# Squares of the out-projections summed on GpSimd, open stage borders and a third weight place in a three-block transformer kernel

## The chip, the cores and the metric

The kernel runs on one core of a Trainium2 chip. The metric is the device time of one execution in microseconds, from its first to its last instruction and what lies around them. Three runs of the kernel before gave 3401.47, 3403.77 and 3406.58 us; their median is 3403.77 us.

## The reference

The program computes two models one after the other on 256 latent tokens of width 2048, in float32. The first has two layers. A layer normalises latent and context tokens (256 each), scales and shifts them by a modulation made from a small vector, projects them by `w_in`, runs grouped-query and latent attention, gates both with a silu, and projects back:

```python
for l in range(DEPTH):
    shift, scale, gate = jnp.split(sc @ w_ada[l] + b_ada[l], 3, axis=-1)
    h_lat = rms_norm(x, norm_g[l]) * (1.0 + scale[:, None]) + shift[:, None]
    ...
    x = x + gate[:, None] * merge_groups(o_a, lat_a[3], o_b, lat_b[3], w_out[l])
return rms_norm(x, final_g)
```

The second model has one layer: a hybrid mixer (forgetting attention and a linear recurrence) with its own out-projection, then an expert layer that picks 128 of 16384 experts for each token. Each norm divides by the root of the mean of the squares over all 2048 channels. Channels lie on the partitions, so that mean is a sum over partitions and over 16 chunks.

## The kernel before

**Stages.** `stages` is a list that every engine walks in the same order. For the first model a layer is: scale, norm, the in-projection (37 weight panels of 1 MB), the grouped attention, the up-projection (7 panels), the latent attention, the out-projection (16 panels). Layer 0 works on 512 columns (context and latent); layer 1 keeps context only where keys and values need it, so most of its outputs have 256 columns. At the start of a stage `begin` (L666) makes an engine wait until the other compute engines have ended all stages before it; each ends a stage with a drain that counts up `done`.

**A weight panel.** SyncE loads it into one of two ring places of 8 KB a partition (`SLOTS`, later six, when the modulation has left its buffers). A panel is split for accuracy: ScalarE rounds half a panel (`act_half`, L1334, instruction at L1345), VectorE subtracts to get the remainder (`dve_half`, L1347, instruction at L1351). There are four places for such halves. TensorE then multiplies hi·hi, hi·lo and lo·hi, 48 matmuls for an output (`pe_output`, L1066, matmuls at L1090). `paced` (L1318) lets ScalarE and VectorE run some halves ahead of the output that they take next. A ring place is free when VectorE has subtracted its second half; SyncE waits for that and issues the next load (L734).

**Modulation.** The products with `w_ada` are done on VectorE, one 1 MB chunk of weights at a time (L1819, 2.3 us each), beside the projections; `ada_after` says how many chunks come behind which output. GpSimd issues their loads into two places (L872) in a hardware loop.

**Norm statistics of an out-projection.** When VectorE has added an output to the residual (L1873), ScalarE squares it into one of two places of `sq` (L1401, or L1394 where two norms are fused and each chunk is squared twice). TensorE multiplies each by a matrix of ones and adds them in PSUM (`sum_squares`, L977, matmuls at L996, or L987 where fused), two outputs behind. There are three such stages: the out-projections of layer 0 (512 columns, 16 sums), of layer 1 (256 columns, fused, 32 sums) and of the second model (256 columns, 16 sums).

**The border behind them.** ScalarE loads an activation table (L1493), takes the root (L1478, L1479), and rounds four weight halves of the next projection before its norm work; VectorE scales each chunk (L1957, or L1955), modulates every fourth itself (L1964), and puts four half subtractions between them; remainders (L1939) run four chunks behind. TensorE starts the next projection with `pe_pair` (matmuls at L1061), two outputs interleaved, each chunk as its remainder is ready.

**Gates.** The last 16 outputs of an in-projection are gates. ScalarE writes each into `sq` place 2 (L1425), stores it to DRAM (L1427) and waits for that store before it writes the next. At the stage's end it waits for all stores.

## Time and profile before

| what | value |
|---|---|
| runs, median | 3403.77 us |
| profiled execution, its own time | 3404.52 us |
| its span | 3402.8 us |
| mean granted clock of TensorE | 0.954 of 2.4 GHz |
| TensorE busy | 89% of the span |
| VectorE, ScalarE, GpSimd busy | 73%, 35%, 18% |
| DMA | 932.69 MB, mean 274 GB/s |

The busy share of TensorE counts overlapping matmuls once, so 89% says that it seldom stands still, not that it runs at its peak. In time, layer 0 lasts to about 1000 us, layer 1 to 1625 us, the mixer and its out-projection to 2037 us, and the expert layer takes the rest.

### The profile page before, as it was taken

The page shows a single profiled execution, that of the slowest core. Times are in us where ns is not written, and L with a number is a line of the kernel's source. Part 1 is how long each engine was busy: PE and PEld are TensorE (multiplying, and loading weights), DVE is VectorE, ACT ScalarE, POOL GpSimd, SP SyncE. Part 2 cuts the span into 40 slices and gives each one's busy share as a digit, 9 for nine tenths or more (in the row PEclk, how much of TensorE's full clock was granted, in tenths as well). Part 3 has the DMA queues.
Part 4 walks back from the last instruction along what each step waited for, and adds up shares of the span by engine and source line. Part 5 has one row for each costly group of instructions (what it writes and reads, how often), then busy time and mean ns, then how long its engine had stood idle before and what let it go on. Part 6 is the DMA issues. An engine that isn't in the chain of part 4 may idle for free.

```text
span 3402.8 us, 39344 instructions
## 1 busy us (share of the span) xinstructions
PE 3036.7 (89%) x14780; PEld 2316.8 (68%) x14780; DVE 2477.8 (73%) x3460; ACT 1174.2 (35%) x1805; POOL 610.7 (18%) x692
## 2 busy tenths in 40 slices
PE   5899999999988998999899999899999997757566
PEld 1577887556767887659899899788888885222223
DVE  7888996655766776547664545598988997888886
ACT  1332323323233333234554635344444443111111
POOL 1000000000100000000000000122122223777773
PEclk9999999999999999999899998999999998878888
DMA  9554674343765676427544444599999999999996
GB/s 407 199 197 183 246 261 174 136 173 139 301 241 222 235 299 258 176 109 283 213 155 145 160 161 151 222 412 419 401 420 399 417 398 381 370 409 409 409 409 264
DMA packets 149479, 932.69 MB, mean 274 GB/s; under 512 B 21552, under 2 KB 30000, under 8 KB 40880
## 3 DMA queue, kind: packets, MB, share of 16 engines
q0 software_dynamic: 77568, 520.24, 39.0%
q1 hardware_dynamic: 57616, 384.82, 28.8%
q10 hardware_dynamic: 14112, 25.17, 1.9%
q8 instruction: 118, 1.93, 0.2%
q14 instruction: 65, 0.53, 0.0%
HBM read 900.79 MB, written 29.36 MB: 273 GB/s over the span
## 4 chain that ended last, share of the span: by engine, by line
PE 56%; DVE 14%; DMA 11%; PEld 7%; issue 6%; POOL 4%; ACT 2%; SPq 0%; DVEq 0%; PEldq 0%; POOLq 0%; ACTq 0%
PE psum L1090 22%; PE psum L1037 16%; PEld psum L1090 7%; PE psum L1099 5%; DMA memh<-dots,memr 4%; DVE w_lo L1351 3%; PE psum L1229 3%; DMA memr<-in_panels_dram 3%; DVE psum L2270 2%; POOL memh L891 2%; PE psum L1246 2%; POOL memr L903 2%; PE psum L1061 2%; DVE junk L1819 2%; DMA memh<-in_panels_dram 1%
## 5 line engine op out<-in xcount | busy, mean ns | idle before, releaser
L1351 DVE TENSOR_TENSOR w_lo<-memr,w_hi 128x1024 fp32r<-128x1024 f32 x614 | 737.0, 1221 | 380.2 <-ACT w_hi L1345 379.6
L1345 ACT ACTIVATE w_hi<-memr 128x1024 fp32r<-128x1024 f32 x614 | 641.0, 1056 | 938.2 <-PE psum L1090 330.9
L1090 PE MATMUL psum<-h_hi,w_hi 128*128 128x512 f32 (+1 forms) x1632 | 587.6, 360 | 19.8 <-DVE w_lo L1351 19.7
L1819 DVE CUSTOM_DVE_ANT_0 junk<-memr 128x2048 bf16<-128x2048 f32 x224 | 512.2, 2287 | 87.4 <-DMA memr<-in_ada_dram 67.1
L1090 PE MATMUL psum<-h_hi,w_lo 128*128 128x512 f32 (+1 forms) x1632 | 563.9, 346 | 0.0
L1090 PE MATMUL psum<-h_lo,w_hi 128*128 128x512 f32 (+1 forms) x1632 | 563.3, 345 | 0.0
L1268 PE MATMUL psum<-memr,memh 128*128 128x512 f32 x576 | 312.6, 702 | 193.1 <-ACT memh L1755 175.7
L1037 PE MATMUL psum<-w_hi,l_hi 128*128 128x512 f32 x1024 | 401.1, 392 | 12.5 <-DVE w_lo L1351 12.4
L1037 PE MATMUL psum<-w_hi,l_lo 128*128 128x512 f32 x1024 | 399.9, 391 | 0.0
L1037 PE MATMUL psum<-w_lo,l_hi 128*128 128x512 f32 x1024 | 399.8, 390 | 0.0
L1268 PEld LDWEIGHTS psum<-memr,memh 128*128 128x128 f32 x576 | 126.0, 226 | 379.3 <-ACT memh L1755 189.3
L1090 PEld LDWEIGHTS psum<-h_hi,w_hi 128*128 128x128 f32 x1632 | 312.0, 191 | 70.2 <-issue 22.1
L1090 PEld LDWEIGHTS psum<-h_lo,w_hi 128*128 128x128 f32 x1632 | 311.9, 191 | 44.9 <-issue 8.8
L872 POOL DMA_DIRECT2D memr<-in_ada_dram x160 | 84.5, 528 | 1433.7 <-DVE mod L1822 1412.7
L1090 PEld LDWEIGHTS psum<-h_hi,w_lo 128*128 128x128 f32 x1632 | 311.6, 191 | 37.1
L2270 DVE SCALAR_TENSOR_TENSOR psum<-memr,memh,psum 128x2048 f32<-128x2048 f32 x118 | 277.9, 2355 | 9.3 <-DVE memr L2207 0.2
L1090 PE MATMUL psum<-l_hi,w_hi 128*128 128x256 f32 x848 | 243.0, 287 | 0.0
L1090 PE MATMUL psum<-l_lo,w_hi 128*128 128x256 f32 x848 | 240.1, 283 | 0.0
L1090 PE MATMUL psum<-l_hi,w_lo 128*128 128x256 f32 x848 | 240.1, 283 | 0.0
L1037 PEld LDWEIGHTS psum<-w_hi,l_hi 128*128 128x128 f32 x1024 | 193.2, 189 | 55.5 <-DVE w_lo L1351 12.6
L882 POOL DMA_INDIRECT memr<-in_peer_u_dram,memr x64 | 76.0, 1188 | 838.7 <-issue 586.7
L1037 PEld LDWEIGHTS psum<-w_lo,l_hi 128*128 128x128 f32 x1024 | 193.1, 189 | 40.2
(273 smaller groups left out, 4475.3 us busy)
## 6 DMA issues: line engine op xcount, KB each, us to landing
memr<-in_panels_dram SPq DMA_DIRECT2D x323, 1024.0 KB, 7.3
memr<-in_ada_dram POOLq DMA_DIRECT2D x168, 1024.0 KB, 6.0
memh<-in_panels_dram SPq DMA_DIRECT2D x16, 1024.0 KB, 23.6
dots<-sq ACTq DMA_DIRECT2D x64, 256.0 KB, 10.0
memh<-in_ada_dram POOLq DMA_DIRECT2D x8, 1024.0 KB, 15.9
memr<-in_xin_dram SPq DMA_DIRECT2D x1, 4096.0 KB, 40.9
gstore<-sq ACTq DMA_DIRECT2D x16, 256.0 KB, 4.8
memh<-gstore SPq DMA_DIRECT2D x2, 2048.0 KB, 7.3
```

The costliest lines, as they stand in the source:

```text
L872: pool.dma_start(adar[:, s_, :], ada[i * 2 + s_]).then_inc(ada_in[s_], 16)
L882: pool.indirect_dma_start(out=early_rows[:, r % EARLY_SLOTS, :], out_offset=None, in_=(peer_u if j < TOPK else peer_v)[:, :], in_offset=ba ...
L891: pool.indirect_dma_start(out=late_act[:, m, j:j + 1], out_offset=None, in_=dots[:, :], in_offset=bass.IndirectOffsetOnAxis(ap=eidx[:, EAR ...
L1037: ins = pe.matmul(bank(2 * (group % 2) + t), x_[:, kc, t * P:t * P + P], u_[:, c, :], start=kc == 0 and j == 0, stop=kc == DC - 1 and j == 2)
L1090: ins = pe.matmul(bank(o["bank"])[:, 0:o["w"]], w_[:, c, :], x_[:, kc, :], start=kc == 0 and j == 0, stop=kc == DC - 1 and j == 2)
L1099: ins = pe.matmul(bank(o["bank"])[:, a:b], lt, rh, start=j == 0, stop=j == len(pairs) - 1)
L1229: ins = pe.matmul(b[:, 0:nk], lt, rh, start=j == 0, stop=j == len(u["s"]) - 1)
L1268: ins = pe.matmul(bank(b), diags[:, q % DIAGS, :], row_views[r % NSLOT][:, 512 * b:512 * b + 512], start=first and i == 0, stop=(EARLY + m ...
L1345: act.activation(w_hi[:, m % HALVES, :, :], slot[:, 8 * i:8 * i + 8, :], ACT.Copy).then_inc(hi_ready, 1)
L1351: dve.tensor_tensor(w_lo[:, m % HALVES, :, :], raw_panel(o["g"])[0][:, 8 * i:8 * i + 8, :], w_hi[:, m % HALVES, :, :].bitcast(F32), ALU.su ...
L1819: chain(dve.tensor_tensor_reduce(junk[:, :], w, cact[:, v_, :], 1.0, 0.0, ALU.mult, ALU.add, mod[:, a, m:m + 1]))
L2270: dve.scalar_tensor_tensor(sums_dve, row, by, sums_dve, ALU.mult, ALU.add).then_inc(row_added, 1)
```

## The change

1. **Squares.** ScalarE writes the squares of the first output straight into `sq` place 2, and GpSimd adds those of outputs 1 to 14 onto them. TensorE sums over partitions twice a norm: the total, and the last output's squares. GpSimd's loop of modulation loads is written out, with the additions placed between the loads.
2. **Borders.** ScalarE and VectorE no longer wait for other engines' `done` at a scale or norm stage behind an out-projection; no engine does at the grouped attention (single semaphores take its place), nor TensorE at an out-projection. Three of the four halves of the next projection are split during the out-projection; one to three halves of an out-projection are split during the latent attention before it (one in layer 0, three in layer 1). The table load moves to the start of the out-projection. VectorE modulates chunks 0, 4, 8, 12 in place of 1, 5, 9, 13, and the remainder of chunk 0 comes behind chunk 2.
3. **Third place.** In layer 1's in-projection, panels go round three places. The third is the context half of `q`, 8 runs of 1 KB a partition, free once the norm has read all of X.
4. **Gates** of 256 columns alternate between the two halves of `sq` place 2; the wait for all stores at the end goes. **Modulation** chunks of layer 1's in-projection are spread anew (the same 42).

```diff
+        for j in range(37):
+            slot_of[first_1 + j] = ((first_1 % SLOTS, (first_1 + 1) % SLOTS, SPARE)[j % 3])
+        spare = region(AR, 8, T2)[:, :, 0:S]
...
-        spread(DC + 60, 42, [0.6] * 2 + [2] * 3 + [0.7] * 12 + [2] * 4 + [0.8] * 14 + [0] * 2)
+        for j, n in enumerate([1, 1, 2, 2, 2] + [1, 1, 0, 1, 1, 1, 1, 1] + [1] * 4 + [2] * 4 + [1] * 15 + [0]):
+            ada_after[DC + 60 + j] = n
...
+            if me in ("act", "dve") and st.get("seam"):
+                upto = 0
+            if me != "sp" and "follows" in st or me == "pe" and "after_split" in st:
+                upto = 0
...
+                    elif slot_of[i] == SPARE:
+                        gr = stages_norm1["groups"][0]
+                        sp.wait_ge(x_out, 16 * nout)
+                        sp.wait_ge(xn_ready, gr["xn"] + len(gr["x"]))
...
+            def add_squares(st, p_):
+                gr = st["sums"]
+                w, per = gr["x"][0].shape[-1], 2 if "fused" in gr else 1
+                for i in range(per):
+                    n = gr["sq0"] + per * p_ + i
+                    pool.wait_ge(sq_ready, n + 1)
+                    if p_ == 0:
+                        pool.sem_inc(sq_used, 1)
+                        continue
+                    total = sq[:, 2, w * i:w * i + w]
+                    if p_ > 1:
+                        pool.wait_ge(sq_used, n - per + 1)
+                    pool.tensor_tensor(total, total, sq[:, n % 2, 0:w], ALU.add).then_inc(sq_used, 1)
...
+            for n in range(DC, N_ADA - DC):
+                o = first_chunk.get(n - 2)
+                while o is not None and added < len(adds) and adds[added][1]["n"] <= o["n"]:
+                    add_squares(adds[added][0], adds[added][2])
+                    added += 1
+                pool.wait_ge(ada_used, n - 1)
+                pool.dma_start(adar[:, n % 2, :], ada[n]).then_inc(ada_in[n % 2], 16)
...
-                if "sums" in st and p_ >= 2:
-                    sum_squares(p_ - 2, p_ - 1)
...
+            if "feeds" in st:
+                halves_ += [(st["feeds"]["outs"][j // 2], j % 2) for j in range(3)]
...
-            if "next" in st and not gs[0].get("early"):
-                for j in range(4):
-                    act_half(act, st["next"]["outs"][j // 2], j % 2)
...
-                        if j in (1, 3, 6, 9) and not gr.get("early"):
-                            n = (1, 3, 6, 9).index(j)
-                            dve_half(dve, st["next"]["outs"][n // 2], n % 2)
-                        if j >= LAG:
+                        if j == 7 and not gr.get("early"):
+                            dve_half(dve, st["next"]["outs"][1], 1)
+                        if j == 2 and not gr.get("early"):
+                            remainder(gr, 0)
+                        if j > LAG or j == LAG and gr.get("early"):
                             remainder(gr, j - LAG)
```

## Rows read from the trace of the kernel before

**Rows 1.** The page, busy time of the engines, and the two groups that split halves.

```profile
PE 3036.7 (89%) x14780; PEld 2316.8 (68%) x14780; DVE 2477.8 (73%) x3460; ACT 1174.2 (35%) x1805; POOL 610.7 (18%) x692
...
L1351 DVE TENSOR_TENSOR w_lo<-memr,w_hi 128x1024 fp32r<-128x1024 f32 x614 | 737.0, 1221 | 380.2 <-ACT w_hi L1345 379.6
L1345 ACT ACTIVATE w_hi<-memr 128x1024 fp32r<-128x1024 f32 x614 | 641.0, 1056 | 938.2 <-PE psum L1090 330.9
```

**Rows 2.** Busy time by stretch (window, length, engines, clock, DMA share, GB/s).

```profile
1023.00:1337.00 314.00, 281.33 (x1824) 255.07 (x1824) 221.66 (x275) 114.29 (x163) 22.17 (x42) 0.98 0.70 268
1515.00:1625.00 110.00, 108.23 (x823) 104.52 (x824) 72.75 (x84) 41.67 (x58) 5.27 (x10) 0.98 0.74 289
...
2148.00:2870.00 722.00, 709.20 (x3136) 585.70 (x3135) 644.52 (x716) 318.71 (x360) 158.97 (x134) 0.99 0.97 396
```

**Rows 3.** Timeline of TensorE, 512-column outputs: sums in layer 0's out-projection.

```profile
976.50 1.02 PE L996 MATMUL psum<-sq,ones 128*128 128x512 f32 x2
...
988.28 1.02 PE L996 MATMUL psum<-sq,ones 128*128 128x512 f32 x2
...
1040.83 0.39 PE L1090 MATMUL psum<-h_hi,w_hi 128*128 128x512 f32 x1
...
1051.71 0.59 PE L964 MATMUL psum<-sq,ones 128*128 128x512 f32 x1
```

**Rows 4.** Timeline of TensorE, 256-column outputs with two, no and one sum.

```profile
1597.23 1.02 PE L987 MATMUL psum<-sq,ones 128*128 128x256 f32 x4
...
1604.04 1.02 PE L987 MATMUL psum<-sq,ones 128*128 128x256 f32 x4
...
1944.53 0.36 PE L1090 MATMUL psum<-m_hi,w_hi 128*128 128x256 f32 x1 [1.50 <-DVE w_lo L1351]
...
1956.12 0.38 PE L996 MATMUL psum<-sq,ones 128*128 128x256 f32 x1
...
1962.30 0.38 PE L996 MATMUL psum<-sq,ones 128*128 128x256 f32 x1
```

**Rows 5.** Timeline at the three borders behind an out-projection.

```profile
1003.42 1.28 ACT L1493 ACT_TABLE_LOAD   x1 [1.62 <-DVEq L2336]
...
1006.20 1.29 DVE L1957 TENSOR_TENSOR memh<-memr,sq 128x512 f32<-128x512 f32 x2 [2.87 <-ACT sq L1479]
...
1013.09 0.77 PE L1061 MATMUL psum<-h_hi,w_hi 128*128 128x512 f32 x1 [10.11 <-DVE h_lo L1939]
...
1638.05 0.55 PE L1061 MATMUL psum<-l_hi,w_hi 128*128 128x256 f32 x1 [9.99 <-DVE l_lo L1939]
...
2046.31 0.55 PE L1061 MATMUL psum<-l_hi,w_hi 128*128 128x256 f32 x1 [7.96 <-DVE l_lo L1939]
```

**Rows 6.** Layer 1's in-projection: TensorE's longest stall, stretches, ScalarE's store wait, panel loads.

```profile
1098.76 0.79 PE L973 MATMUL psum<-memr,consts 128*128 128x256 f32 x1 [10.53 <-DVE memr L1918]
...
1076.00:1175.00 99.00, 82.19 (x620) 79.05 (x619) 72.67 (x99) 38.63 (x65) 6.33 (x12) 0.95 0.70 266
1221.00:1331.00 110.00, 100.15 (x774) 95.39 (x772) 77.37 (x86) 42.33 (x51) 8.45 (x16) 0.98 0.83 320
...
ACT sq L1425 <- DMA gstore<-sq: 12.8, 5, 6.5
...
memr<-in_panels_dram SPq DMA_DIRECT2D x15, 1024.0 KB, 7.6
```

**Rows 7.** Timeline of TensorE's starts: attention in layers 0 and 1, out-projections.

```profile
556.75 0.65 PE L1229 MATMUL psum<-memr 128*128 128x256 f32 x1 [2.83 <-ACTq L1804]
...
812.22 0.76 PE L1090 MATMUL psum<-h_hi,w_hi 128*128 128x512 f32 x1 [4.79 <-DVE w_lo L1351]
...
1337.51 1.22 PE L1229 MATMUL psum<-memr 128*128 128x512 f32 x1 [6.79 <-ACTq L1804]
...
1515.39 0.36 PE L1090 MATMUL psum<-h_hi,w_hi 128*128 128x256 f32 x1 [4.04 <-DVE w_lo L1351]
```

**Rows 8.** Groups of VectorE, 815 to 1000 us: the modulation chunks.

```profile
L1819 DVE CUSTOM_DVE_ANT_0 junk<-memr 128x2048 bf16<-128x2048 f32 x32 | 73.2, 2286 | 24.0 <-DMA memr<-in_ada_dram 24.0
```

More of the change, by code:

```diff
@@ L195, in build @@
         gate_st = sq
+        gate_at = [sq[:, i, :] for i in range(3)] + [sq[:, 2, S * i:S * i + S] for i in range(2)]
         prob = sq
@@ L521, in build @@
             summed = gemm(g, DC, out_proj)
+            first = summed["outs"][0]["half"]
+            mla["feeds"], summed["after_split"] = summed, 8 * (layer + 1)
+            summed["ahead"] = next(i for i in range(HALVES) if (first + i) % HALVES == HALVES - 1)
+            first_x["panels"] = summed["ahead"] // 2
             g += DC
@@ L660, in build @@
         early = [gr for st in stages if st["kind"] == "norm" for gr in st["groups"] if gr.get("early")]
+        stages_norm1 = next(st for st in stages if st["kind"] == "norm" and st["groups"][0]["a"] == ADA0[1])
         def ended(e, k):
@@ L1088, in pe_output @@
                             pe.wait_ge(xl_ready, chunks + kc + 1)
+                        if split is not None and half == 1:
+                            pe.wait_ge(y_split, split - 7 + c)
                         for j, (w_, x_) in enumerate(((wh, xh), (wh, xl), (wl, xh))):
@@ L1227, in score @@
                     pe.wait_ge(exp_ready, u["n"] - 2)
+                if "follows" in st and u is us[0]:
+                    pe.wait_ge(roped, max(gr["sw"] for gr in st["follows"]["inside"] if "rope" in gr) + 1)
+                    pe.wait_ge(normed, max(gr["ms"] for gr in st["follows"]["inside"]) + 1)
+                    for e in ("V", "A"):
+                        pe.wait_ge(evac[e], max(o["ev"] for o in st["follows"]["outs"] if o["eng"] == e and "gate" not in o) + 1)
+                if "follows" in st and u in us[0:3]:
+                    emptied(S_BANK + u["n"] % 3)
                 for j, (lt, rh) in enumerate(u["s"]):
@@ L1443, in act_gemm @@
             n_gates = max([o["gate"] + (2 if "dense" in o else 1) for o in st["outs"] if "gate" in o], default=0)
-            if n_gates:
+            if n_gates and "inside" not in st:
                 for i in sorted(set(gate_slot[:n_gates])):
```

172 lines of the change are left out of this document (115 added, 57 removed).

## The prediction

> **What bounds it now.** I read the page first: TensorE is busy 89% of the span, VectorE 73%, GpSimd 18% [rows 1]. Then the stretches, stage by stage. Behind 2148 us stands the expert layer, with DMA at 97% of its engines and 396 GB/s [rows 2]; nothing there is edited, and its first loads hang on the work before it, so I let all that is gained earlier reach the end one for one. Before it the chain of waits runs mostly on TensorE. So a microsecond counts where TensorE works on less, or stands still less. The timeline of TensorE shows where it stands: 2.8 to 6.8 us at the starts of the grouped attention and of the out-projections [rows 7], 8 to 10 us behind each out-projection [rows 5], and, scattered, in layer 1's in-projection [rows 6]. Last I compared neighbouring outputs with and without sums of squares [rows 3, 4].
>
> **Squares.** Layer 0: an output with its sum takes 988.28 - 976.50 = 11.78 us, one without 1051.71 - 1040.83 = 10.88 us [rows 3]. Thirteen of the 16 sums stand between outputs (two outputs behind), so 13 x 0.90 = 11.7 us is the ceiling; the last ones wait for ScalarE's last square in either kernel and give nothing. Layer 1: 6.81 us with two sums, 5.80 us without (1956.12 - 1944.53, over two) [rows 4], a ceiling of 13 x 1.01 = 13 us. Second model: 1962.30 - 1956.12 = 6.18 against 5.80 [rows 4], 13 x 0.38 = 5 us.
>
> What comes in are 14 additions of 512 columns, 28 of 256 and 14 of 256 on GpSimd. No row shows GpSimd computing. From below the bound is VectorE's own pass over 512 columns, 1.29/2 = 0.65 us [rows 5]. From above only the stage gives one: layer 1 has 5.8 us for its two additions of 256 columns, so from 5.8 us for 512 columns on the stage would feel it (rival d). I take 1.3 us, twice the lower end, and 0.7 us for 256 columns, since GpSimd has one instruction where VectorE streams. ScalarE's squares have room: they wait for GpSimd, one output behind, not for TensorE, two behind.
>
> Do these additions cost VectorE anything? The trace before cannot show it. At zero cost layer 1's 110 us stage, in which VectorE is busy 72.75 us [rows 2], shrinks to 97 us and VectorE fits. If every addition held VectorE up for its length, 28 x 0.7 = 20 us would come to 72.75, and 92.4 us in a stage of 97, with every dependent wait on top, is no fit. I take 5 us of layer 1's 13. In layer 0 the modulation takes 73.2 us and VectorE waits 24.0 us more for its loads [rows 8]; these loads now stand behind the additions in GpSimd's queue. An addition is asked for some 2 us after the output, and there are over 10 us between outputs, so I take 10 of 11.7. The second model has no modulation left: all 5. The Trainium skill speaks against this part (SBUF — State Buffer, "Who interferes with whom"): a VectorE instruction with two SBUF inputs and a GpSimd instruction that reads SBUF exclude each other for their whole length. The half subtractions and the modulation are of that kind; by that rule layer 1 gains about nothing from the squares, and the sum below is 5 us smaller. No run here shows it yet.
>
> **The three borders behind out-projections.** Now, at the first: the table load takes 1.28 us after a drain [rows 5], then root and exponential, VectorE's first chunk at 1006.20, TensorE's first matmul at 1013.09. After: the load is gone from this place (1.3 us, and 0.4 us of drains). Behind VectorE's start come two scaled chunks and a modulation, then two half subtractions of 1.2 us [rows 1], then more; now it is one scaled and modulated chunk, two more scaled, and the remainder: 5 x 0.65 = 3.3 us in place of 6.9. Together TensorE starts 5.2 us sooner. It then starves until chunk 4, since remainders 1 to 3 still wait for later scaling, so I take 4.5 us. At the second (fused) border columns are half as many: 2.0 us in place of 5.3, plus table, drains and a double square less at the end of the chain: 5.9 us, and three 1.2 us halves less in VectorE's 16 chunks, which there set the pace: 7 us. At the third likewise: 4.9 us sooner, 6.5 us in all. The clock goes the same way: the first matmul after the stall lasts 0.77 us and the same shape later 0.39 us [rows 3, 5], the lower and the full level, after TensorE had stood still 10 us. Their three halves move into the out-projection's last two outputs, 3 x (1.1 + 1.2) us on ScalarE and VectorE [rows 1] beside 5.8 to 10.9 us of matmuls for an output. If that cover were gone, the 3.6 us on VectorE would show once a border.
>
> **Starts of attention and out-projection.** Grouped attention now waits for single semaphores. Layer 1: TensorE stood still 6.79 us behind a ScalarE that waited for the store of the gate before [rows 6, 7]; with two places and no wait for stores that goes, and the slow clock of its first scores: 7 us. The third exponential now waits for the last two stores, and the gates' reload for all stores; I take both as hidden by the units before them. Layer 0: 2.83 us [rows 7], of which the table load behind the last gate keeps some: 2.5 us. Out-projections: 4.79 and 4.04 us [rows 7] go, since the first half is split and the first eight chunks are rounded before the attention ends. The second half of the panel is needed 24 matmuls later (5.4 us in layer 0), and two splits take 2.3 us [rows 1]. With the clock kept I take 6 and 5.5 us. The halves inside the attention cost nothing: TensorE, not ScalarE or VectorE, paces it; without that cover they are 1 to 3 times 1.2 us.
>
> **Layer 1's in-projection,** the largest term. Two stretches. From 1076 to 1175 us, 12 outputs of 256 columns in 99 us: at 5.80 us they need 70, and some 21 sums and rotations of 256 columns at half a microsecond (a double one costs 1.01 [rows 4]) 11 more, so 18 us are lost, 10.53 of them in one stall of a rotation behind VectorE, which waited for modulation [rows 6]. From 1221 to 1331 us, 16 gates in 110 us against 16 x 5.80 = 93: 17 us lost. Cause: a place turns round in a load (7.6 us to landing [rows 6]), two roundings (2.1) and one subtraction (1.2) [rows 1], 11 us and up to one modulation of 2.3 us in VectorE's way, some 13.5 us; two places give a panel every 6.8 us, three every 4.5 us. Store waits of 12.8 us on ScalarE [rows 6] also go. The next limit is DMA: a gate moves 1 MB of panel, 1 MB of modulation and 0.13 MB of store, 2.2 MB in 5.8 us, 385 GB/s, against the 396 GB/s that the chip holds behind 2148 us [rows 2]. So the gates settle near 6.0 us: 13 us. In the first stretch VectorE is busy 72.67 of 99 us [rows 6]; I give it back 11 of 18. The third place fills late, only when the norm has read all of X, while TensorE is on the first pair: up to 2 us lost. Together 22 us; bounds 8 (only the store waits) and 35.
>
> **Sum.** 10 + 5 + 5 (squares) + 4.5 + 7 + 6.5 (borders) + 2.5 + 7 + 6 + 5.5 (starts) + 22 = 81 us. The profiled execution took 3404.52 us, 0.75 above the median, so 3323.5 us; against the median 3323. Forecast: 3324 us.
>
> **Rivals.**
> (a) GpSimd in VectorE's way. Squares give 8 in place of 20, and late modulation takes 5 of the borders' gain: 3404.5 - 64 = 3340 us. For it: both work on SBUF all the time in these stages, and VectorE already waits 24.0 us for loads in layer 0. Against: in layer 0 it has room.
> (b) The third place does not pay, because DMA or VectorE stands behind it at once: 8 in place of 22, 3338 us; with (a), 3352. For it: 385 of 396 GB/s leaves little. Against: the stretch moved 320 GB/s [rows 6].
> (c) All of the ceilings: 35 for the in-projection, 13 for layer 1's squares: 3303 us.
> (d) Slower than before. One mechanism: GpSimd's additions so slow that they set the out-projections' pace, through `sq_used` and the squares behind it. With X us for 512 columns, X/2 for 256, a loss of 14 (X - 10.9) + 14 (X - 5.8) + 14 (X/2 - 5.8) = 35 X - 315 us stands against 61 us that are left of the gain: from X = 10.7 us on it is slower; at 12 us, 3449 us. That is 16 times VectorE's pass [rows 5], and the Trainium skill (GPSIMD Engine Reference, "Elementwise — side-by-side cycle accounting") puts the ratio near 2; by it (d) is out, and an addition of 512 columns is about 1.3 us.
> (e) The change doesn't do what it says: borders stay closed since something else ends last there. At the out-projections that would be the second half's split; then 11 us of starts stay: 3335 us.
>
> **Chances.** Forecast 0.45, (a) 0.2, (b) 0.15, (c) 0.08, (e) 0.09, (d) and other losses 0.03. All but (d) lie far beyond 0.2% (6.8 us), about what a measurement of this kernel can tell from no change: faster 0.95, within 0.01, slower 0.04. The range takes (c) and (a), (b) and (e) alone, with part of (a) and (b) together: 3303 to 3349 us.
>
> **What would show it.** The lines of sums shrink to 4, 8 and 4 matmul records; outputs in layer 0 follow at 10.9 us, in layer 1 at 6 to 6.8 us. GpSimd shows additions; if half subtractions beside them last over 1.25 us, or stand behind them, (a) holds. TensorE starts 5 us after the roots at the borders, in place of 8 to 10. The gates take 16 x 6.0 us. Wrong would be: gates still at 6.9 us, VectorE waiting over 40 us for modulation in layer 0, or an expert layer longer than its 722 us.

## The result, and the profile after

The changed kernel takes 3328.1 us in the median of four runs (3326.6 to 3329.3), the kernel before 3404.2 (3401.5 to 3406.6) beside it: a ratio of 0.978, 95% interval 0.977 to 0.979, 76 us shorter. The forecast was 3324 us, with 3303 to 3349 around it. The profiled execution has a span of 3325.5 us.

The page after, the lines that answer to [rows 1]:

```profile
PE 2998.3 (90%) x14668; PEld 2290.7 (69%) x14668; DVE 2492.4 (75%) x3460; ACT 1174.1 (35%) x1804; POOL 704.6 (21%) x748
...
L1437 DVE TENSOR_TENSOR w_lo<-memr,w_hi 128x1024 fp32r<-128x1024 f32 x614 | 744.1, 1233 | 330.5 <-ACT w_hi L1430 330.1
L1430 ACT ACTIVATE w_hi<-memr 128x1024 fp32r<-128x1024 f32 x614 | 642.5, 1057 | 873.4 <-PE psum L1150 383.9
```

TensorE has 112 matmul records less and is busy 38 us less; the other 39 us of the span were idle time. GpSimd has 56 instructions and 94 us more, VectorE 15 us more for the same 3460 instructions.

The stretches of the kernel after (window, length, busy time of TensorE, its weight loads, VectorE, ScalarE and GpSimd, granted clock, DMA share, GB/s): layer 0's out-projection, the two parts of layer 1's in-projection, layer 1's out-projection, the second model's.

```profile
802.75:985.10 182.35, 177.61 (x769) 146.17 (x770) 139.06 (x162) 45.51 (x51) 51.78 (x46) 0.98 0.78 300
1057.90:1207.60 149.70, 140.71 (x920) 128.43 (x919) 116.46 (x155) 55.48 (x86) 11.61 (x22) 0.99 0.72 271
1207.60:1288.80 81.20, 81.20 (x674) 80.77 (x672) 65.86 (x72) 36.23 (x44) 7.39 (x14) 1.00 0.95 360
1464.60:1560.80 96.20, 94.87 (x769) 93.04 (x770) 79.53 (x85) 45.44 (x64) 53.78 (x38) 1.00 0.82 312
1866.40:1966.40 100.00, 96.64 (x769) 96.14 (x770) 59.90 (x81) 44.91 (x60) 10.37 (x14) 0.95 0.53 191
```

The third row shows the third panel place at work: 14 gates in which TensorE never stops, all but the first 5.76 us apart, where [rows 6] had 6.9; DMA is at 0.95. The last eleven outputs of the three out-projections follow at 10.88, 6.10 and 5.76 us in the mean (11.78, 6.95 and 6.18 before). The last row also prices an addition of 256 columns by itself: 10.37/14 = 0.74 us.

The ends of TensorE's stalls, from its timeline (start, length, line, in brackets the idle time before and what ended it): the starts of [rows 7], then the borders of [rows 5].

```profile
552.31 0.89 PE L1301 MATMUL psum<-memr 128*128 128x256 f32 x3 [0.36 <-issue]
802.75 0.47 PE L1150 MATMUL psum<-h_hi,w_hi 128*128 128x512 f32 x1 [0.26 <-issue]
1289.47 2.81 PE L1301 MATMUL psum<-memr 128*128 128x512 f32 x6 [0.62 <-ACT sq L1508]
1464.62 0.36 PE L1150 MATMUL psum<-h_hi,w_hi 128*128 128x256 f32 x1 [0.25 <-issue]
...
993.06 0.76 PE L1119 MATMUL psum<-h_hi,w_hi 128*128 128x512 f32 x1 [5.07 <-DVE h_lo L2047]
1570.14 0.55 PE L1119 MATMUL psum<-l_hi,w_hi 128*128 128x256 f32 x1 [5.39 <-DVE l_lo L2047]
1971.33 0.39 PE L1119 MATMUL psum<-l_hi,w_hi 128*128 128x256 f32 x1 [3.25 <-DVE l_lo L2047]
```

All seven are shorter, as forecast. New places of loss, and one that stayed, in the same columns (the last pair in the second model's out-projection):

```profile
842.39 2.29 DVE L1927 CUSTOM_DVE_ANT_0 junk<-memr 128x2048 bf16<-128x2048 f32 x1 [4.88 <-DMA memr<-in_ada_dram]
846.13 0.80 PE L1150 MATMUL psum<-h_hi,w_hi 128*128 128x512 f32 x1 [4.70 <-DVE w_lo L1437]
...
1074.07 1.22 PE L1039 MATMUL psum<-memr,consts 128*128 128x256 f32 x2 [3.98 <-DVE memr L2026]
1116.81 0.70 PE L1039 MATMUL psum<-memr,consts 128*128 128x256 f32 x2 [0.72 <-DVE memr L2026]
...
1295.96 0.69 ACT L1654 ACTIVATE sq<-psum,stat 128x512 f32<-128x512 f32 x1 [3.66 <-DMA gstore<-sq]
1297.60 0.63 PE L1311 MATMUL psum<-consts,sq 128*128 128x128 f32 x4 [2.95 <-DVE sq L2109]
...
1873.49 1.28 ACT L1521 ACT_TABLE_LOAD   x1 [0.67 <-DVEq L2449]
1877.35 0.56 PE L1150 MATMUL psum<-m_hi,w_hi 128*128 128x256 f32 x1 [3.25 <-DVE w_lo L1437]
```

Layer 0's out-projection now stands still 4.70 us in its third output, behind a VectorE that waited for a modulation row. In layer 1's q stretch the outputs follow at 7.59 us, each with 0.72 us ahead of the swap L1039, exactly as before. The third exponential of layer 1's attention waits 3.66 us for a gate's store, which costs TensorE 2.95 us. And in the second model the activation table, which is now loaded at the start of the out-projection, stands directly ahead of weight halves that TensorE waits for: the stall there is 3.25 us, 1.50 before [rows 4], and the stage got only 1.4 us shorter (101.4 to 100.0).

### The profile page after: what moved, and what is told of

Its sections match the earlier page's. It is cut to its first block, busy times and chain, and to the rows that moved or that the text cites. A ratio compares the mean times of both kernels' runs of the same rounds, so it can differ in the third digit from the quotient of the medians.

```text
span 3325.5 us, 38664 instructions
## 1 busy us (share of the span) xinstructions
PE 2998.3 (90%) x14668; PEld 2290.7 (69%) x14668; DVE 2492.4 (75%) x3460; ACT 1174.1 (35%) x1804; POOL 704.6 (21%) x748
## 3 DMA queue, kind: packets, MB, share of 16 engines
q8 instruction: 117, 1.92, 0.2%
## 4 chain that ended last, share of the span: by engine, by line
PE 66%; DVE 12%; DMA 8%; issue 5%; POOL 5%; ACT 2%; DVEq 0%; SPq 0%; ACTq 0%; POOLq 0%
PE psum L1150 31%; PE psum L1095 17%; PE psum L1159 6%; DMA memh<-dots,memr 3%; PE psum L1301 3%; DVE w_lo L1437 3%; POOL memr L969 2%; PE psum L1119 2%; POOL memh L957 2%; PE psum L1320 2%; DVE psum L2383 2%; DMA memr<-in_panels_dram 2%; DMA memh<-in_panels_dram 1%; DVE junk L1927 1%; PE psum L1342 1%
## 5 line engine op out<-in xcount | busy, mean ns | idle before, releaser
L1150 PE MATMUL psum<-h_hi,w_hi 128*128 128x512 f32 (+1 forms) x1632 | 576.9, 354 | 6.6 <-DVE w_lo L1437 6.0
L1927 DVE CUSTOM_DVE_ANT_0 junk<-memr 128x2048 bf16<-128x2048 f32 x224 | 520.6, 2324 | 75.5 <-DMA memr<-in_ada_dram 54.9
L1095 PE MATMUL psum<-w_hi,l_hi 128*128 128x512 f32 x1024 | 400.0, 391 | 12.9 <-DVE w_lo L1437 12.8
L1095 PEld LDWEIGHTS psum<-w_hi,l_lo 128*128 128x128 f32 x1024 | 192.9, 188 | 40.0
```

The source lines that it names most:

```text
L1095: ins = pe.matmul(bank(2 * (group % 2) + t), x_[:, kc, t * P:t * P + P], u_[:, c, :], start=kc == 0 and j == 0, stop=kc == DC - 1 and j == 2)
L1150: ins = pe.matmul(bank(o["bank"])[:, 0:o["w"]], w_[:, c, :], x_[:, kc, :], start=kc == 0 and j == 0, stop=kc == DC - 1 and j == 2)
L1927: chain(dve.tensor_tensor_reduce(junk[:, :], w, cact[:, v_, :], 1.0, 0.0, ALU.mult, ALU.add, mod[:, a, m:m + 1]))
```

## The experiments

Each is the kernel after with one edit, but for "whole old norm" and "three mends", which join several. The medians, and against the kernel after's 3328.1 us:

| run | median us (range) | ratio to before, 95% | against after |
|---|---|---|---|
| sums back on TensorE | 3354.5 (3353.1–3356.1) | 0.986 (0.984–0.987) | +26.3 |
| two panel places | 3343.5 (3338.2–3345.7) | 0.982 (0.981–0.984) | +15.4 |
| one store place | 3330.6 (3329.8–3335.8) | 0.979 (0.977–0.980) | +2.4 |
| closed borders | 3328.8 (3326.3–3330.0) | 0.978 (0.976–0.979) | +0.7 |
| old modulation spread | 3328.8 (3326.6–3330.8) | 0.978 (0.976–0.979) | +0.6 |
| count, don't add | 3333.0 (3330.3–3334.3) | 0.979 (0.978–0.981) | +4.9 |
| fewer early chunks | 3325.5 (3322.7–3328.3) | 0.977 (0.975–0.978) | −2.7 |
| swap bank freed early | 3318.5 (3317.3–3324.5) | 0.975 (0.973–0.976) | −9.6 |
| halves in the norm | 3335.5 (3332.4–3337.1) | 0.980 (0.979–0.982) | +7.4 |
| whole old norm | 3341.1 (3334.9–3342.1) | 0.982 (0.980–0.983) | +13.0 |
| three mends | 3314.7 (3312.9–3318.7) | 0.975 (0.973–0.976) | −13.4 |
| closed starts | 3333.8 (3330.7–3334.0) | 0.980 (0.978–0.981) | +5.7 |

The ranges are up to 8 us wide, so of these differences 0.6, 0.7, 2.4 and −2.7 can't be told from nothing. The kernel before, run beside each, had its median at 3404.2 us, but at 3402.5 beside halves in the norm, whole old norm and three mends; measured from there these three would stand some 1.8 us higher. A stage is read from one profiled execution each, and two stages differ between executions where the code is the same: layer 0's out-projection takes 179.2 to 182.4 us, and layer 1's grouped attention (from the last gate to the up-projection) 38.9 to 45.6 us, at a granted clock of 0.92 to 1.00.

**Sums back on TensorE.**

```diff
-                while o is not None and added < len(adds) and adds[added][1]["n"] <= o["n"]:
-                    add_squares(adds[added][0], adds[added][2])
-                    added += 1
...
+                if "sums" in st and p_ >= 2:
+                    sum_squares(p_ - 2, p_ - 1)
...
-                sum_squares()
+                sum_squares(len(st["outs"]) - 2, len(st["outs"]))
```

> The kernel after, with the additions taken from GpSimd: ScalarE's squares go to two buffers and TensorE sums each over the partitions between outputs again, as before the change. Open borders, early weight halves and the third panel place stay. Theory A (the sums between outputs stalled TensorE by a microsecond or less each in the first model's out-projections, and their removal is worth about what was forecast): 8 to 11 us longer in layer 0, 5 to 8 in layer 1, 1 to 5 in the second model, so 3346 us (3342 to 3352). Rival B (most of the 5.6 and 13.0 us that the out-projections gained came from the early starts, and GpSimd's hold on VectorE pays the rest back): 3328 to 3336 us, with layer 0's stage not longer than 184 us.

The three out-projections of this run, columns as above:

```profile
803.15:993.30 190.15, 188.17 (x795) 150.26 (x796) 131.16 (x162) 45.49 (x51) 16.91 (x32) 0.99 0.74 288
1471.70:1577.60 105.90, 105.90 (x821) 102.58 (x822) 72.01 (x84) 43.47 (x60) 5.29 (x10) 1.00 0.77 289
1887.00:1992.10 105.10, 101.70 (x795) 100.57 (x796) 59.90 (x80) 44.73 (x59) 0.00 (x0) 0.96 0.50 182
```

They are 7.8, 9.7 and 5.1 us longer than after, and the second border, with its double sum, is 3.6 us longer (first pair after it ends 30.3 us behind the last matmul, 26.8 in the kernel after). Theory A, and more than it: the squares are worth 26 us, not 20. (The first and the third border are 0.9 and 1.0 us shorter in this run, so the stages' differences come to 24 us.) Layer 0's 7.8 us hold a smaller stall of the third output, 1.92 for 4.70 us; between later outputs the sum costs its full 0.90 us (11.78 for 10.88). In layer 1 TensorE is busy 105.90 of 105.90 us, so there the sums are plain work and nothing hides them.

**Two panel places; one store place.**

```diff
-            slot_of[first_1 + j] = ((first_1 % SLOTS, (first_1 + 1) % SLOTS, SPARE)[j % 3])
+            slot_of[first_1 + j] = (first_1 + j) % SLOTS
```

> The kernel after, with the 37 panels of layer 1's in-projection in two places in turn, no third. Theory A (the third place is what brings the gate outputs from 6.9 to 5.8 us each): 11 to 13 us back in the gates, and the stall at the start of the stage from 4.0 to about 10 us, so 17 us longer (13 to 22), 3345 us, gate outputs at 6.8 to 7.0 us. Rival B (the gates came to 5.8 us because their stores have two places and the third panel place adds little): at most 5 us longer, gate outputs at 5.8 to 6.1 us.

The gates' stretch of this run:

```profile
1206.10:1298.20 92.10, 85.07 (x674) 81.52 (x672) 67.22 (x72) 36.57 (x45) 7.33 (x14) 1.00 0.86 326
```

10.9 us longer than the 81.20 us above, and the outputs before are 3 us longer. The last twelve gates lie 6.5 to 7.4 us apart instead of 5.76; the DMA share falls from 0.95 to 0.86. That is theory A for the gates. Its second half fails: the second output of the stage takes 10.9 us here too (17.3 before), so the early stall has another cause.

```diff
-                            gate_slot.append(n % 3 if "dense" in o else 2 if o["w"] == T2 else 3 + n % 2)
+                            gate_slot.append(n % 3 if "dense" in o else 2)
```

> The kernel after, with every gate output of layer 1 stored from one place again instead of two in turn. Theory A (a store lands 1.7 to 5.2 us after its issue, within the 5.8 us of an output): 0 to 3 us longer, 3330 us, gates at 5.8 to 5.9 us each. Rival B of the run with two panel places (the store place was the bound): 10 us or more longer, gates at 6.5 us or more.

Theory A, 2.4 us longer: nearly all gates stay at 5.76 us, single ones take 6.1, 6.7 and 8.2. The 12.8 us of store waits of [rows 6] were mostly hidden before and are no term of their own.

**Closed borders, halves in the norm, whole old norm.**

```diff
-            st = stage("norm", groups=groups, engines=("pe", "act", "dve"), seam=bool(groups[0].get("summed")))
+            st = stage("norm", groups=groups, engines=("pe", "act", "dve"))
```

(and the same in the three calls for the scale stages: without the mark `seam`, ScalarE and VectorE wait at the entry again)

> The kernel after, with the three borders between a projection and the next norm closed: VectorE and ScalarE enter the scale and norm stages only when all engines have ended the stage before. The new order of modulation and rounding inside the norm, the early halves, and the attention's and out-projections' open starts stay. Theory A (the waits at the border are what was saved there): 3 borders by 2 to 4 us, so 9 us longer (6 to 13), 3337 us, each border from the last out-projection matmul to the end of the pair 2 to 4 us longer. Rival B (what was saved comes from the order inside the norm and the weight halves made beforehand): at most 3 us longer.

The first matmul of the first pair in this run:

```profile
989.00 0.77 PE L1119 MATMUL psum<-h_hi,w_hi 128*128 128x512 f32 x1 [5.35 <-DVE h_lo L2047]
```

0.28 us more idle than after (0.26 and 0.20 at the other two), 0.7 us in all, no difference that can be measured. Theory A falls: that the borders are open is worth nothing that can be measured. ScalarE's first work behind the entry, the logarithm, needs TensorE's last sum in either case (in the kernel after it starts 0.2 us behind it). So the next two runs asked what did shorten them.

```diff
-                    st["groups"][0]["summed"]["feeds"] = nxt
...
+            if "next" in st and not gs[0].get("early"):
+                for j in range(4):
+                    act_half(act, st["next"]["outs"][j // 2], j % 2)
...
-                        if j == 7 and not gr.get("early"):
-                            dve_half(dve, st["next"]["outs"][1], 1)
+                        if j in (1, 3, 6, 9) and not gr.get("early"):
+                            n = (1, 3, 6, 9).index(j)
+                            dve_half(dve, st["next"]["outs"][n // 2], n % 2)
```

> The kernel after, with the first four weight halves behind each of the three borders made inside the norm again: four ScalarE copies of 0.97 us right behind the root, as before the change. Closing the borders had cost nothing, so something else shortened them by 3.0, 5.0 and 5.3 us. Theory A (it was these four copies, which stood before the first rounding of the norm, and the table load of 1.28 us ahead of the logarithm): each border 3.5 to 4 us longer, 3339 us (3336 to 3342), the start of the pair at 11.5 to 12 us behind the last matmul in border 1. Rival B (it was the new order of modulation and rounding): at most 1 us per border, 3331 us.

ScalarE behind the first root, and the first matmul of the first and the third pair:

```profile
985.20 0.63 ACT L1562 ACTIVATE sq<-sq 128x512 f32<-128x512 f32 x1
985.73 3.88 ACT L1428 ACTIVATE w_hi<-memr 128x1024 fp32r<-128x1024 f32 x4
989.52 0.61 ACT L1602 ACTIVATE h_hi<-memh 128x512 fp32r<-128x512 f32 x1
...
991.00 0.77 PE L1117 MATMUL psum<-h_hi,w_hi 128*128 128x512 f32 x1 [6.70 <-DVE h_lo L2046]
...
1977.96 0.55 PE L1117 MATMUL psum<-l_hi,w_hi 128*128 128x256 f32 x1 [6.07 <-DVE l_lo L2046]
```

The borders, to the end of the pair, are 2.2, 2.7 and 3.2 us longer. Four copies, 3.88 us, now stand ahead of the first rounding, which comes 4.32 us behind the start of the root instead of 2.26: some 1.8 us of them lie in a time in which ScalarE waited for VectorE's first scaling and modulation anyway. That is between the theories, nearer to A.

```diff
-            return c % 2 == 1 if gr.get("early") else c % 4 == 0
+            return c % (2 if gr.get("early") else 4) == 1
...
-            if "sums" in st:
-                act.preload_act_table_set("natural_log_exp_and_others")
...
+            act.preload_act_table_set("natural_log_exp_and_others")
```

(with the edits of the two runs before, and the norm's loops of before on both engines)

> The kernel after with everything of the three borders as before the change: halves in the norm, the old order of modulation and rounding, the table loaded inside the norm, borders closed. Theory A: the halves carry 10 to 12 us (the run before), the table load 1.3 us per border, the order about nothing, so 14 to 16 us over the kernel after, 3343 us. Rival B (the order carries most): 5 us or more above the run with the halves alone.

```profile
988.03 1.28 ACT L1574 ACT_TABLE_LOAD   x1 [1.62 <-DVEq L2446]
...
997.70 0.77 PE L1117 MATMUL psum<-h_hi,w_hi 128*128 128x512 f32 x1 [10.11 <-DVE h_lo L2045]
...
1887.20 0.36 PE L1148 MATMUL psum<-m_hi,w_hi 128*128 128x256 f32 x1 [1.55 <-DVE w_lo L1435]
```

The first border is back at [rows 5] to a hundredth: 10.11 us idle, 40.8 us to the end of the pair. The whole costs 13.0 us. That is 5.6 us above the run with the halves alone, which would just meet rival B's figure, but the two runs' ranges overlap (3334.9 to 3342.1 and 3332.4 to 3337.1), and the traces don't bear it out: against that run the three borders are 0.9 and 1.4 us longer and, the second, 0.5 us shorter, 1.8 us in all, and most of the rest lies in the two stages named above that differ between executions. So at the borders the halves carry 8.1 us, table load and order about 2. The last line shows the other side of the table load: with it back in the norm, the second model's out-projection stalls 1.55 us instead of 3.25 and takes 95.9 us, where the eleven other profiles without sums on TensorE take 98.6 to 100.4.

**Closed starts.**

```diff
-            st["follows"] = in_st
...
-            mla["feeds"], summed["after_split"] = summed, 8 * (layer + 1)
+            mla["feeds"] = summed
...
-            if n_gates and "inside" not in st:
+            if n_gates:
```

> The kernel after, with the two layers' attention and out-projection entered only when all engines have ended the stage before (for the attention: when the last gate store has landed as well), but with the out-projection's first weight halves still made during the attention. The run with closed borders cost nothing; this asks the same of the four starts. Theory A (as in the forecast, the waits at these starts are worth about what the trace shows: L0's attention 2.4 us, L1's 5.1 us; the out-projections' gap goes from 0.25 to about 2 us because the last head's remainder has to end first): 10 us longer (7 to 13), 3338 us. Rival B (here too the halves made beforehand are all of it): at most 3 us longer, 3331 us.

```profile
554.14 0.48 PE L1300 MATMUL psum<-memr 128*128 128x256 f32 x1 [2.82 <-ACTq L1911]
...
806.05 0.47 PE L1149 MATMUL psum<-h_hi,w_hi 128*128 128x512 f32 x1 [2.26 <-DVEq L2448]
845.40 0.50 PE L1149 MATMUL psum<-h_hi,w_hi 128*128 128x512 f32 x1 [1.02 <-DVE w_lo L1436]
...
1292.58 1.22 PE L1300 MATMUL psum<-memr 128*128 128x512 f32 x1 [6.30 <-ACTq L1911]
```

The gaps at the attentions are nearly those before the change (2.82 and 6.30 us), those at the out-projections less than half of it (2.26, and 1.52 in layer 1). Together 11.4 us more idle than after, for 5.7 us of time, between the two theories. In layer 0 the start that comes 2 us later is given back: the stall of the third output is 1.02 us and the stage 175.7 us. In layer 1 the attention itself is 1.0 us shorter, though its clock is 0.93: with all stores landed, the third exponential has none to wait for.

**Old modulation spread.**

```diff
-        for j, n in enumerate([1, 1, 2, 2, 2] + [1, 1, 0, 1, 1, 1, 1, 1] + [1] * 4 + [2] * 4 + [1] * 15 + [0]):
-            ada_after[DC + 60 + j] = n
+        spread(DC + 60, 42, [0.6] * 2 + [2] * 3 + [0.7] * 12 + [2] * 4 + [0.8] * 14 + [0] * 2)
```

> The kernel after, with the modulation chunks of layer 1's in-projection spread over its outputs as before the change (1, 0, 3, 2, 3, 1 in the first six instead of 1, 1, 2, 2, 2, 1). The run with two panel places showed the stage's second output at 10.9 us where the kernel before has 17.3, so the third place is not what shortened it. Theory A (the three chunks at once in the third output kept VectorE from the second weight half): the second output is back at 13 to 17 us and the kernel 3 to 7 us longer, 3332 us. Rival B (the weight halves made at another point of the norm shortened it): second output at 10.5 to 11.5 us, within 2 us of the kernel after.

The second output takes 15.0 us, with 8.24 us of stall at the swap of 1076.66 where after has 3.98, and the stage is 5.8 us longer: theory A on the spot. But the kernel is only 0.6 us longer. The attention behind it takes 37.7 us instead of 40.5: its third exponential waits 0.5 us for the gate's store instead of 3.66. The rest is lost over several stages. So the new spread's gain in the stage hardly reaches the end.

**Count, don't add.**

```diff
-                    pool.tensor_tensor(total, total, sq[:, n % 2, 0:w], ALU.add).then_inc(sq_used, 1)
+                    pool.sem_inc(sq_used, 1)
```

> The kernel after, with GpSimd counting each square as used without adding it up: this leaves out all but the first and the last output's squares of each norm's sum, so that what the additions themselves cost can be read. Theory A (an addition holds VectorE for 0.84 us at most, and VectorE has room for it in three of the four places): 0 to 4 us shorter, 3326 us, layer 0's out-projection 0 to 3 us shorter than the kernel after. Rival B (the additions delay the modulation rows behind them in GpSimd's queue, and so make the stall of 2.6 to 4.7 us in layer 0's third output): that stall is gone, and the kernel 4 to 8 us shorter.

Both theories fail: without the additions the kernel is longer. Layer 0's stage is at 179.2 us, with 2.6 us of its stall left, just as in three runs with additions (two panel places, closed borders, halves in the norm: 179.2 to 179.3 us, stall 2.6 to 2.7), so the additions don't make that stall. Layer 1's out-projection takes 102.6 us, while in the eleven profiles with additions it takes 96.1 to 97.5. TensorE, VectorE and ScalarE there (groups: count, busy us, mean ns, idle before):

```profile
L1150 PE MATMUL psum<-h_hi,w_hi 128*128 128x256 f32 x256 | 73.4, 287 | 8.0 <-DVE w_lo L1437 7.8 <-issue 0.3
L1437 DVE TENSOR_TENSOR w_lo<-memr,w_hi 128x1024 fp32r<-128x1024 f32 x31 | 37.3, 1220 | 29.3 <-ACT w_hi L1430 29.3
L1430 ACT ACTIVATE w_hi<-memr 128x1024 fp32r<-128x1024 f32 x32 | 33.2, 1050 | 28.2 <-DMA memr<-in_panels_dram 28.2
```

and the same stage after:

```profile
L1150 PE MATMUL psum<-h_hi,w_hi 128*128 128x256 f32 x256 | 73.8, 288 | 1.6 <-DVE w_lo L1437 1.3 <-issue 0.3
...
L1437 DVE TENSOR_TENSOR w_lo<-memr,w_hi 128x1024 fp32r<-128x1024 f32 x31 | 45.1, 1472 | 14.3 <-ACT w_hi L1430 14.2
L1430 ACT ACTIVATE w_hi<-memr 128x1024 fp32r<-128x1024 f32 x32 | 33.4, 1051 | 18.2 <-DMA memr<-in_panels_dram 18.2
```

VectorE's subtractions are faster without the additions, 1220 against 1472 ns, and still TensorE waits 6.5 us more for them, since ScalarE waits 10 us more for panels, whose median landing goes from 5.3 to 7.9 us. The modulation rows' own landing is 5.5 us instead of 7.1. What differs is when GpSimd issues the rows' loads. After:

```profile
1487.40 3.93 POOL L922 TENSOR_TENSOR sq<-sq 128x256 f32<-128x256 f32 x2 [1.51 <-ACT sq L1479]
1491.28 0.56 POOL L936 DMA_DIRECT2D memr<-in_ada_dram  x1
```

and without the additions:

```profile
1493.82 0.53 POOL L936 DMA_DIRECT2D memr<-in_ada_dram  x1 [8.78 <-DVE mod L1930]
```

With additions the modulation load is issued behind them, 2.0 us after VectorE's release (0.3 us without). That is enough to change the order: with additions the panel's load goes first (1490.77, the row 1491.28), without them the row's (1493.82, the panel 1494.68). A panel that TensorE needs in 6 us then lands behind a row that has time. The landing times and the order of issue are measured; that the order alone makes the 6 us was not tried with a pause in the place of an addition. The run with the sums back on TensorE issues its rows early too, and its panels land in 5.9 us; there an output takes 6.81 us and TensorE waits for none of them.

**Fewer early chunks; the swap's bank; three mends.**

```diff
-        spread(DC + 44, 32, [1] * 14 + [0] * 2)
+        for j, n in enumerate([1, 2, 2, 2, 3, 2, 2, 3, 2, 3, 2, 3, 2, 3, 0, 0]):
+            ada_after[DC + 44 + j] = n
```

> The kernel after, with layer 0's out-projection taking 1, 2, 2, 2, 3, 2, 2, 3, ... modulation chunks in place of 2, 3, 2, 2, 2, 3, ...: two fewer in its first two outputs. Theory A (VectorE waits there for a modulation row that lands late behind the 4 MB of x, and the third output's low half is late with it): the stall of 2.6 to 4.7 us before the third output is gone, and the kernel 2 to 7 us shorter, 3324 us. Rival B (what is late there is the third panel itself, behind x): the stall stays at 2 us or more and the time within 2 us of the kernel after.

The stall is gone: the stage takes 175.2 us, 7.2 less than after (4.7 of stall, the rest the slower clock behind it: granted 0.98 over the stage, now 1.00). Theory A in the stage; the kernel's 2.7 us are within the ranges, since 4.2 us come back at the border. ScalarE at the stage's end:

```profile
979.17 1.06 ACT L1431 ACTIVATE w_hi<-memr 128x1024 fp32r<-128x1024 f32 x1 [3.55 <-DMA memr<-in_panels_dram]
982.30 0.63 ACT L1485 ACTIVATE sq<-memr 128x512 f32<-128x512 f32 x1 [2.08 <-DVE memr L1982]
```

The third half made beforehand stands ahead of the last output's squares, and its panel, whose place the last output frees, is late once the stage is fast: the price of work pulled across a border.

```diff
-                        pe.wait_ge(roped, gr["sw"])
...
+                        pe.wait_ge(swap_read, n_read)
...
-                    dve.tensor_tensor(t, t, con(sin, S), ALU.mult)
+                    dve.tensor_tensor(root1, t, con(sin, S), ALU.mult).then_inc(swap_read, 1)
```

> The kernel after, with the first step of a rotation inside the in-projections written to SBUF and not back into the one PSUM bank, so that TensorE's next swap waits only for VectorE's first reading and not for the whole rotation. Theory A (the outputs at 7.59 us in layer 1's q stretch, each with a gap of 0.72 us ahead of the swap, are a loop through VectorE's scaling and rotation): the gap is gone, six to eight outputs at 6.6 to 6.9 us, and the kernel 5 to 8 us shorter, 3321 us. Rival B (the loop is through the weight halves and TensorE waits for VectorE's root product anyhow): outputs stay at 7.4 us or more, the kernel within 2 us.

```profile
1111.37 0.70 PE L1041 MATMUL psum<-memr,consts 128*128 128x256 f32 x2
1118.18 0.70 PE L1041 MATMUL psum<-memr,consts 128*128 128x256 f32 x2
```

6.81 us apart instead of 7.59, no idle time ahead of the swap, and the stage 5.5 us shorter. Theory A. The median gains 9.6 us, the profiled span only 3.0: that execution is the slowest of its four (3324.5 us, the others 3317.3 to 3319.1), its grouped attention in layer 1 is 3.1 us longer at a clock of 0.92, its expert layer 3.3 us longer. The stage's 5.5 us are what the edit is sure of.

```diff
+            late = "feeds" in st and "sums" in st
...
-                while j < min(2 * split + (5 if "x" in o else 4), len(halves_)):
+                while j < min(2 * split + (5 if "x" in o else 4), len(halves_) - late):
...
+            if late:
+                part(*halves_[-1])
```

(with the edits of the two runs before)

> The kernel after with three mends: the swap's bank freed at VectorE's first reading (9.6 us shorter alone), layer 0's out-projection with 1, 2, 2, 2, 3, ... chunks (2.7 us alone, because 4.3 us of its 7 came back at the next border, where ScalarE stood 3.6 us for a panel ahead of the last output's squares), and, for that, the third weight half of the next projection made behind the last output's squares instead of ahead of them. Theory A (the wait for the panel then lies beside the last squares' way): border 1 at 36 to 38 us beside a stage of 175 to 176 us, 3314 us (3311 to 3318). Rival B (the panel is simply that late, and the pair waits for it): border 1 at 40 us or more, 3318 us.

```profile
976.85 0.63 ACT L1490 ACTIVATE sq<-memr 128x512 f32<-128x512 f32 x1 [3.19 <-DVE memr L1987]
977.39 1.04 ACT L1436 ACTIVATE w_hi<-memr 128x1024 fp32r<-128x1024 f32 x1
978.84 0.69 ACT L1569 ACTIVATE sq<-psum,eps_t 128x512 f32<-128x512 f32 x1 [0.41 <-PE psum L1058]
```

The half now lies between the last squares and the logarithm, where ScalarE waits for TensorE anyway. Layer 0's stage takes 175.3 us and the border behind it 37.5: theory A. At 3314.7 us this version beats both kernels, by 13.4 and by 88 us.

## Why the prediction was right, and where its steps were not

The total was right, 76 us for 81, and the third place, the largest term, was right in size and reason. Stage by stage the two traces differ like this; to the right is what a run that undoes one part gave alone:

| stage | forecast us | traces, before less after | alone, by a run |
|---|---|---|---|
| layer 0, start of the attention | 2.5 | 3.0 | all four starts: 5.7 |
| layer 0, out-projection (squares 10, start 6) | 16 | 10.2 | squares 7.8 |
| first border | 4.5 | 3.1 | all three: 13.0 (opening 0.7, halves 7.4) |
| layer 1, in-projection | 22 | 23.7 | third place 15.4 |
| layer 1, start of the attention | 7 | 5.1 | |
| layer 1, out-projection (squares 5, start 5.5) | 10.5 | 16.8 | squares 9.7 |
| second border | 7 | 5.0 | of it squares 3.6 |
| second model, out-projection (squares) | 5 | 1.4 | squares 5.1 |
| third border | 6.5 | 5.3 | |
| all else | 0 | 3.9 | |

In sum 81 and 77.3 us. That the total came so near is in part luck: layer 0's out-projection, the borders, layer 1's attention and the second model's out-projection gave 16 us less than forecast, and the other stages 12 more, 4 of them where nothing was forecast.

**Squares: mis-sized in layer 1, 5 for 9.7 us.** I gave back 8 of 13 us because additions might hold VectorE up. They do, but only a little. In layer 0 (kernel after) the 14 additions last 2.50 us in the mean. VectorE and GpSimd at one of them, and the last one, beside a VectorE that is idle until 979.39:

```profile
955.77 3.12 DVE L1927 CUSTOM_DVE_ANT_0 junk<-memr 128x2048 bf16<-128x2048 f32 x1
...
954.15 2.60 POOL L922 TENSOR_TENSOR sq<-sq 128x512 f32<-128x512 f32 x1 [5.03 <-ACT sq L1484]
...
978.49 1.29 POOL L922 TENSOR_TENSOR sq<-sq 128x512 f32<-128x512 f32 x1 [2.54 <-ACT sq L1484]
```

An addition takes 1.29 us alone, the 1.3 of the forecast. The first one shown begins inside the modulation pass before (953.32 to 955.60) and ends 1.15 us behind it, and the next pass lasts 3.12 us instead of 2.28: the two take turns. Of layer 0's 32 passes ten last 3.11 us or more. By the Trainium skill (SBUF — State Buffer, "Who interferes with whom") they exclude each other for whole instructions, and the trace agrees; but VectorE loses 0.84 us an addition here, not the addition's length, since the addition spends the first part of its 2.60 us beside the pass that was already under way. The term that I drew from "no fit" (20 us on VectorE in layer 1) was 7.8: 31 subtractions at 1472 instead of 1220 ns. By the sign that I had set for it (half subtractions over 1.25 us) the mechanism of rival (a) is there; its price is not, for the squares gave 26 us and not 8. (Rival (a) with (b) was mis-added: 3404.5 less 50 us is 3354, not 3352.) Rival (d) is out at 1.29 us an addition.

**The second model: squares right, a term missing.** The sums were worth 5.1 us for the 5 forecast, but the stage gave 1.4. The step that failed is the table load, "gone from this place": I put what the table load costs in its new place at nothing. There it stands ahead of three weight halves, the stall grows from 1.50 to 3.25 us, and the clock over the stage falls from 0.98 to 0.95; with the load back in the norm the stage takes 95.9 us, 3 to 4 us less. The one table load, moved, cost most of what the squares brought there.

**Borders: right about the work, wrong about the waits.** The time came mostly from the three halves made beforehand, as the sum was worked out. But it was 13.4 us, not 18, and 3.6 of it are the second border's sums, which the run with the sums back counts too. "TensorE starts 5.2 us sooner" held at the first border: 4.9 us, from the last matmul of the out-projection to the first of the pair; and at the third, 4.7 for 4.9. What failed at the first is the price of "it then starves until chunk 4": 0.7 us in the forecast, 1.9 in the trace, where the pair takes 29.8 us instead of 27.9. At the second TensorE starts 4.1 us sooner, for 5.9 forecast. At the last two the pair itself is only 0.8 and 0.6 us shorter, for 1.1 and 1.6. Rival (e), "borders stay closed", was true where I had not put it: here a closed entry costs nothing that can be measured.

**Starts: over-sized in layer 0's out-projection.** From the end of the attention to the end of the out-projection it went from 192.8 to 182.6 us, 10.2 for 16 with the squares, of which those are 7.8; the start gave 2.4 us for 6. What failed is "with the clock kept I take 6": the gap of 4.79 us went and one of 4.70 us took its place 43 us later, with 2.5 us of slower clock behind it. I had named nobody who would be late next there; it was VectorE, with a row of modulation issued while x was loading. In layer 1 the 13.0 us of the stage and the 3.8 of the gap are 9.7 us of squares, 3.8 of gap and 3.3 us that the run with the sums back keeps (stage 105.9 us, 109.2 before, without the small stalls and at a clock of 1.00 for 0.98); so this start gave 7 us for 5.5, and the early halves, which I take for the reason, were not undone alone. Layer 1's attention gave 5.1 instead of 7: "I take both as hidden", of the third exponential's wait for the last two stores, was wrong by 2.95 us. (That attention stretch differs by up to 7 us between executions, so its 5.1 us are rough.)

**In-projection: right in sum and shares, with one limit not seen.** The last twelve gates went from 84.4 to 69.3 us, 15 for the 13 of the forecast, since they came to 5.76 us and not to 6.0: at 360 GB/s, DMA share 0.95, the queue still kept up. The part before gave 8.6 us for the 9 forecast. The undoing run gives the third place 10.9 of the gates' 15 us. In the part before 6.6 us of the long stall went, 4.3 by the new spread, while the loop at 7.59 us stayed whole. I had explained this part by modulation in VectorE's way alone; the run with the bank freed early shows that each output also waited for a rotation through a single bank.

The runs that undo one part add to 26.3 + 15.4 + 2.4 + 0.6 + 13.0 + 5.7 = 63.4 of the 76.1 us. The early halves of the out-projections were not undone alone; the gaps of the run with closed starts (2.26 and 1.52 us for 4.79 and 4.04) give them 5 us. What is left, some 8 us, remains unassigned; 2.0 of it lie before layer 0's attention, where nothing was forecast, and 1.3 in the expert layer.

## What to carry to other kernels

A closed border costs only what its engines could have done during it: first move work (weight halves) out of it, and open it after. See where moved work lands: a table load of 1.28 us taken out of three borders stood, at one of the three, ahead of halves that TensorE waited for, and cost 3 to 4 us there. Put work that is pulled across a border behind the last instruction that the border itself waits for. Before moving work to another engine, ask what that engine's queue issues behind it: here the additions delayed loads that had time, and the run without them was 4.9 us longer although VectorE's subtractions were faster.

## What the runs showed of the hardware

- A GpSimd addition of 512 columns (two operands in SBUF) takes 1.29 us, of 256 columns 0.74; VectorE's pass over 512 columns takes 0.65 us [rows 5]. The Trainium skill (GPSIMD Engine Reference, "Elementwise — side-by-side cycle accounting") puts the ratio near 2, and the trace agrees.
- Beside VectorE's modulation passes (two operands) it takes 2.6 us in 13 of layer 0's 14 additions, and the pass behind it 3.12 instead of 2.28 us. Beside the additions of 256 columns the half subtractions take 1.47 instead of 1.22 us in the mean.
- Loads on two queues share the engines: with modulation rows issued 0.9 us ahead of the panels instead of 0.5 us behind them, the panels' median landing went from 5.3 to 7.9 us and the rows' from 7.1 to 5.5, for the same 30 MB of the stage.
- After a stall of 4.70 us TensorE's first matmul of 512 columns lasted 0.80 us and those at the full clock 0.39; the stage lost 2.5 us on top of the stall (in the run with the bank freed early 1.3 us, behind a stall of 4.77).
- The granted clock of one stretch of the same code differs between executions: layer 1's grouped attention ran at 0.92 to 1.00.
